# Two transformer blocks on one core: the upper level products of the first block's recurrence, asked for one weight block later

## What is computed

```python
# recurrence (HGRN2), per head, keys and values 128 wide
f = lb + (1 - lb) * sigmoid(f_raw);  k = 1 - f;  q = silu(q_raw);  v = i_raw
S_t = diag(f_t) S_{t-1} + k_t outer v_t;   o_t = S_t^T q_t
o = o * rsqrt(mean(o * o) + EPS) * norm_w * silu(g_raw)
# attention: a mixture of three dilated causal windows over the same 256 tokens
o_att = sum over branches of softmax weights times v
mixed = concat(o_rec, o_att) @ w_out
```

## Time and profile before

| | |
|---|---|
| median of 3 runs | 1996.77 us (1995.89 to 1997.70) |
| span of the profiled execution, first to last instruction | 1994.8 us |
| TensorE busy | 1841.5 us (92% of the span) |
| VectorE busy | 1394.3 us (70%) |
| ScalarE busy | 903.3 us (45%) |
| GpSimd busy | 709.3 us (36%) |
| mean granted TensorE clock | 0.958 |

### The profile page before, as it was taken

One profiled execution on the slowest core, in us unless ns is written; L12 is line 12 of the kernel. 1 busy time (PEld: TensorE's weight loads), 2 busy tenths in 40 slices (PEclk: granted clock), 3 DMA queues, 4 the chain that ended last, 5 costly groups with the idle time before them and its releaser, 6 DMA issues.

```text
span 1994.8 us, 29743 instructions
## 1 busy us (share of the span) xinstructions
PE 1841.5 (92%) x10284; PEld 1600.5 (80%) x10284; DVE 1394.3 (70%) x1633; ACT 903.3 (45%) x1160; POOL 709.3 (36%) x612
## 2 busy tenths in 40 slices
PE   5899999999987999999999999998999587899997
PEld 4777888788876888888888888887888466788886
DVE  7866866667747877777777644446786887778854
ACT  4444444344435555555555433335554233345532
POOL 3444432244494211111111111224451999600033
PEclk9899999999997999999999999999999798899998
DMA  6333444333642455555545455554454233344452
GB/s 253 124 132 134 160 147 147 126 141 133 255 166 105 171 188 189 189 187 186 183 183 188 177 188 186 185 185 177 161 180 175 85 126 108 141 167 153 169 189 105
DMA packets 50424, 326.49 MB, mean 164 GB/s; under 512 B 5840, under 2 KB 6480, under 8 KB 17744
## 3 DMA queue, kind: packets, MB, share of 16 engines
q1 hardware_dynamic: 50384, 325.96, 45.6%
HBM read 323.84 MB, written 2.10 MB: 163 GB/s over the span
## 4 chain that ended last, share of the span: by engine, by line
PE 67%; DVE 12%; POOL 12%; issue 5%; ACT 2%; DMA 1%; POOLq 1%; DVEq 0%; SPq 0%; ACTq 0%
PE ps L1587 42%; PE ps L1588 22%; POOL lev_in L1460 3%; POOL pfx L1464 2%; POOL lev_in L1456 2%; DVE wlo L835 2%; POOL sfx L1463 2%; POOL sq L1479 1%; DVE act_a L1074 1%; ACT whi L429 1%; POOL mem_again L1428 1%; DVE eq L858 1%; PE ps_sc L1626 1%; DVE ef L858 1%; DVE act_a L878 1%
## 5 line engine op out<-in xcount | busy, mean ns | idle before, releaser
L1587 PE MATMUL ps<-act_a,whi 128*128 128x512 f32 x3136 | 1147.9, 406 | 56.5 <-DVE tmp L841 23.9
L1588 PE MATMUL ps<-act_a,wlo 128*128 128x256 f32 x3136 | 900.3, 287 | 0.0
L835 DVE TENSOR_TENSOR wlo<-stage,whi 128x2048 fp32r<-128x2048 f32 (+1 forms) x317 | 721.5, 2276 | 232.5 <-ACT whi L429 228.2
L1587 PEld LDWEIGHTS ps<-act_a,whi 128*128 128x128 f32 x3136 | 605.8, 193 | 203.3 <-issue 33.8
L429 ACT ACTIVATE whi<-stage 128x2048 fp32r<-128x2048 f32 (+1 forms) x317 | 571.2, 1802 | 121.8 <-DMA stage<-in_w_down 108.2
L1588 PEld LDWEIGHTS ps<-act_a,wlo 128*128 128x128 f32 x3136 | 606.3, 193 | 0.7
L1587 PE MATMUL ps<-big,whi 128*128 128x512 f32 x1600 | 568.8, 397 | 8.5 <-DVE big L1165 6.9
L1588 PE MATMUL ps<-big,wlo 128*128 128x256 f32 x1600 | 454.6, 284 | 0.0
L436 ACT ACTIVATE small<-ps 128x256 f32<-128x256 f32 x252 | 96.7, 384 | 624.3 <-PE ps L1588 624.2
L1587 PEld LDWEIGHTS ps<-big,whi 128*128 128x128 f32 x1600 | 303.0, 189 | 79.6 <-DVE big L1165 5.2
L1588 PEld LDWEIGHTS ps<-big,wlo 128*128 128x128 f32 x1600 | 303.3, 190 | 0.1
(11 more groups left out here) (326 smaller groups left out, 1475.0 us busy)
## 6 DMA issues: line engine op xcount, KB each, us to landing
stage<-in_w_a SPq DMA_DIRECT2D x167, 1024.0 KB, 4.8
stage<-in_w_b SPq DMA_DIRECT2D x87, 1024.0 KB, 4.8
stage<-in_w_down SPq DMA_DIRECT2D x64, 704.0 KB, 4.0
h<-in_xT SPq DMA_DIRECT2D x8, 512.0 KB, 6.4
mem_raw<-in_memT SPq DMA_DIRECT2D x1, 2048.0 KB, 10.7
mem_again<-in_memT SPq DMA_DIRECT2D x4, 512.0 KB, 7.4
out<-o_out SPq DMA_DIRECT2D x4, 512.0 KB, 2.7
stage<-in_w_a SPq DMA_DIRECT2D x4, 256.0 KB, 7.0
```

Source lines behind the costliest of these rows:

```text
L835: dve.tensor_tensor(wlo[:, slot, part], stage[:, slot, part], whi[:, slot, part].bitcast(F32), ALU.subtract).then_inc(w_lo, 1)
L1587: pe.matmul(ps[:, bank, :], whi[:, slot, c * P:(c + 1) * P], act, start=start, stop=False)
L1588: return pe.matmul(ps[:, bank, T:2 * T], wlo[:, slot, c * P:(c + 1) * P], act[:, 0:T], start=False, stop=stop)
```

## The change

Three engines' orders are changed; no instruction is added, removed or resized.

- TensorE: in the middle heads, levels 4 to 7 and the cross product now come behind block 6 in place of ahead of it. Head 7 takes the order that head 0 has: inside block 6, behind 12 of its cells. Head 0 keeps its order.
- VectorE, in all heads: the masked copies of levels 4 to 7 (and in head 0 the second half of the memory splits) move from behind the attention's maxima to behind block 6's add, block 9's residual and the scaling of the output gate.
- ScalarE, in all heads: the copy of the cross product moves from ahead of the exponentials of the scores to behind block 6's evacuation, block 9's conversion and the exponential of the output gate; that exponential moves ahead of the copy of `avtok`.

```diff
@@ scalar, mixers_head
                 hi(start, i, 8, 8)
 
-                wait(act, "lev_ready", i * 5 + 5)
-                act.activation(sT[:, P:2 * P], ps_cross, ACT.Copy).then_inc(s("cross_ready"), 1)
-
                 wait(act, "att_max", i + 1)
...
                 evac(u + 6, b)
                 if not last:
                     hi(start, i, 8, 9)
+                wait(act, "hg_lin", i + 1)
+                act.activation(eg[:, :], hgx[:, :], ACT.Exp, scale=-1.0).then_inc(s("hg_exp"), 1)
+                wait(act, "lev_ready", i * 5 + 5)
+                act.activation(sT[:, P:2 * P], ps_cross, ACT.Copy).then_inc(s("cross_ready"), 1)
                 wait(act, "av_turned", i + 1)
                 act.activation(avtok[:, :, :], ps_t[:, 0:T].rearrange("p (a b) -> p a b", a=2), ACT.Copy).then_inc(s("avtok_ready"), 1)
-                wait(act, "hg_lin", i + 1)
-                act.activation(eg[:, :], hgx[:, :], ACT.Exp, scale=-1.0).then_inc(s("hg_exp"), 1)
@@ vector, mixers_head
-                place_levels(i, range(4, LEVELS))
-                if first:
-                    mem_lo(1)
                 add(u + 6, b)
                 if memory:
                     lo(start, i, 8, 9)
                 scaled(u + 6, b, hgx[:, :], "hg_lin")
+                place_levels(i, range(4, LEVELS))
+                if first:
+                    mem_lo(1)
@@ tensor, mixers_head
-                if not first:
+                if memory:
+                    whole(start, i, 8, 6, u + 6, b, act_a)
                     levels(i, range(4, LEVELS + 1))
-                if first:
+                else:
                     await_block(start, i, 8, 6, u + 6)
                     cells((start + 6) % NS, b, act_a, range(3 * KT // 4), closes=False)
                     levels(i, range(4, LEVELS + 1))
                     cells((start + 6) % NS, b, act_a, range(3 * KT // 4, KT), opens=False).then_inc(w_used, 1)
-                else:
-                    whole(start, i, 8, 6, u + 6, b, act_a)
```

## The result

The changed kernel takes 1953.74 us (median of 4 runs, 1951.92 to 1954.98), the kernel before 1997.24 (4 runs). The ratio is 0.9779, with a 95% interval of 0.9765 to 0.9793. That is 43.5 us less, where 42.7 were forecast: 1953.7 against 1954.1. The span of the profiled execution went from 1994.8 to 1950.9 us, by 43.9.

The account below looks back on a forecast made before the run. TensorE's waits for GpSimd's chain of decays were taken to bound the first block's heads. Middle heads 43.8, head 0 -3.3 and head 7 2.2 sum to 42.7 us saved, so 1954.1 us, range 1949 to 1966.

Parts of the forecast that it names:

- The bound of the stage: First block's heads: TensorE waits for GpSimd's chain of decays, idling 3.51 and 0.91 us in the third middle head.
- The sum of a middle head: Heads 1 to 6, scores to hg_out: seven terms sum to 14.21 us without waits; gain 43.8 us over six heads.
- The two small covers: Middle heads: inputs ready before TensorE asks, by 0.3 us at the cross product and 0.4 us at hg_out.
- The split of the gain: Each middle head's 7.3 us: 4.4 idle time, 2.9 matmuls no longer run at the lower clock.
- Head 0: First head: hg_out moves to 84.65, losing 2.5 us, plus 0.8 for clock and VectorE's lateness; cost 3.3 us.
- Head 7: Last head: gain 3.1 us less 0.9 for slow cells, so 2.2 us, with some 2.5 us waiting before hg_out.
- What is behind: Steps after head 7, MLP included: lengths unchanged, the saving carried to the end.
- the first (the wait moves to hg_out): Middle heads: missing hg_out's cover by 1 to 2.5 us each gives 1960 to 1969 us; chance 0.11.
- The second (GpSimd last again): Middle heads: one more VectorE-GpSimd collision makes GpSimd's chain last, 10 us back, 1964 us; chance 0.06.
- The third (the clock stays down): Middle heads: slow matmuls stay without idle time, half to all of 17 us back, 1963 to 1971 us; chance 0.05.
- the fifth (VectorE sets the period): Middle heads: products asked for later but the period stays, set by VectorE; 1997 us; chance 0.02.
- The fourth: Middle heads: a wait at hg_out over 7.7 us each makes it slower, 2005 us at 9 us; chance 0.02.

Follow-up runs that it names:

- the two delays: Changed kernel with one extra ScalarE operation ahead of block 6's evacuation in middle heads: a 600-column copy, 1953.67 us; a 128-column logarithm, 1960.13 us.
- the three quarter form: Changed kernel with middle heads in head 7's form, levels 4 to 7 and cross product behind 12 of block 6's 16 cells: 1965.27 us.
- The filled kernel: Kernel before, with unread identity transposes where TensorE would wait, 31 ahead of level 7 and 14 ahead of the cross product: 1986.45 us.

## Why the prediction was right, step by step

- *The bound of the stage.* Right. With TensorE's order alone the gain is all there; with the order of the others alone there is none.
- *The sum of a middle head.* 14.21 us were put together from seven rows of before, 14.10 were measured, and the gain was 44.2 for 43.8. No wait came up. The largest difference in one term is 0.1 us, in scores and block 6 together (6.27 for 6.36). The two small covers were right: the cross product came at 7.99 with its input at 7.66 (cover 0.33 for 0.3), and the two delays put the cover of hg_out at 0.37 and 0.40 (0.4). They and the three quarter form show that these covers are real edges: what is lost past them is lost in every middle head.
- *The split of the gain.* Wrong, though the total doesn't hang on it. The text gave 4.4 us per head to idle time and 2.9 to the clock. The filled kernel shows 5.2 and 2.1 (5.4 and 2.1 in heads 2 to 6). The step that failed was to take the idle time of the trace as the cost of the wait. Level 7 ran at the lower clock inside the wait for the cross product's input, in 1.12 us for 0.42; at the full clock TensorE would only have waited 0.7 us longer there. Another 0.24 us is that the profile counts the idle time from the modelled end of the levels before (240.80 + 1.50 = 242.30), while the next work could have started at 0.65 + 1.26 = 1.91 us after the scores, which is 242.06. The wait costs the distance from the work's end to the input's arrival at the full clock, 7.7 less 2.3 us of work, and that is 5.4 (4.4 + 0.7 + 0.24).
- *Head 0.* The wait was forecast to the tenth (hg_out at 84.65, measured 84.72). The 0.8 us for the clock and VectorE's lateness measured 0.5: of the next block 4 cells ran at the lower clock where 2 had before.
- *Head 7.* 3.1 us was 3.15. The allowance of 0.9 for slow cells was too small: behind the 2.5 us wait the granted clock was 0.79 in place of 1.00, and hg_out with the 14 cells took 1.4 us more.
- *What is behind.* Right: the MLP again has no gap, at clock 1.00, and everything behind the heads took 1496.6 us for 1497.5.
- *The total.* The gain of the span is 1.2 us more than the forecast of 42.7. Of that 0.95 is the scatter behind the heads; the misses of the parts (+0.3 in head 0, +0.4 in the middle heads, -0.5 at head 7) nearly cancel.
- *What the prediction didn't see.* It costed the new order of VectorE and ScalarE in heads 0 and 7, 3.3 us and the wait in head 7, but took it as the price of the middle heads. It never asked what those would do without it. That was about 6 us left lying, and TensorE's order alone is as fast as any kernel here (1947.37 us; 1947.38 with the old order in heads 0 and 7).

Of the rivals, the first (the wait moves to hg_out) happened in heads 0 and 7 only, where the sum had it. The second (GpSimd last again) needed 0.33 us more and didn't come; the three quarter form is the picture of it. The third (the clock stays down) and the fifth (VectorE sets the period) fall with the period of 51.87 us at clock 1.00 and VectorE busy for 41.07 of it. The fourth would have needed a delay over 7 us.

## What to carry to other kernels

Where one engine waits in program order for another's chain, compare the end of the chain with the work that could stand in front of the wait; when one unit of that work covers it, move the wait behind it. Here the sum from single rows was good to about a tenth of a microsecond per head. Test each engine's reordering by itself: here the waiting engine's move brought everything, and the matching moves of the others brought nothing and cost time in heads 0 and 7, where no whole block was left to hide them. The idle time that a trace shows can be less than what a wait costs, when matmuls inside the wait run at the lower clock. A kernel with only one of the two taken away tells how much each is.

## What was not expected of the hardware

- Transposes of the identity that nobody reads, in place of the idle time, were enough to hold the granted clock at 1.00 over the whole period of a head, at 0.11 us each from start to start (14 from 246.01 to 247.54). Where the same kernel waited without them, 3.64 us in head 1, matmuls of 512 columns took 0.63 us again behind the wait.
- A wait of under a microsecond can lower the clock or leave it: with three quarters of a block, head 3 had granted clock 0.90 over the stretch and the five other middle heads 1.00. The wait was 0.97 us in head 3, and 0.95 to 0.97 in the others, so its length doesn't set them apart. What does isn't settled; all had the same work in front.
